# RWKV recurrence: four more two-bank products copied out of PSUM by ScalarE and VectorE, one bank each

## What is computed

```python
def step(state, inp):                      # per token, 4 heads of 64
    r_t, w_t, k_t, v_t, kk_t, b_t = inp
    sa = jnp.einsum("bhvk,bhk->bhv", state, -kk_t)
    state = (state * w_t[:, :, None, :] + sa[..., None] * b_t[:, :, None, :]
             + v_t[..., None] * k_t[:, :, None, :])
    y_t = jnp.einsum("bhvk,bhk->bhv", state, r_t)
    return state, y_t
_, y = lax.scan(step, s0, (tm(rh), tm(wh), tm(kh), tm(vh), tm(kk), tm(bh)))
ym = jnp.mean(y, axis=-1, keepdims=True)
yv = jnp.mean(jnp.square(y - ym), axis=-1, keepdims=True)
y = (y - ym) * lax.rsqrt(yv + GN_EPS) * gn_w + gn_b
```

## Time and profile before

| | |
|---|---|
| runs | 2478.01, 2481.12, 2484.82 us |
| profiled execution | 2481.37 us, span 2479.6 us, mean granted clock 0.923 |
| RWKV recurrence in it | about 455 to 696 us |
| busy in the whole span | TensorE 87%, VectorE 34%, ScalarE 24%, GpSimd 9% |

### The profile page before, as it was taken

The page is one execution under the profiler, slowest core; times in us unless marked ns, Lnnn a source line. Parts: engine busy times, 40 slices in busy tenths (PEclk is TensorE's granted clock), DMA queues, the critical chain, the costliest instruction groups (busy, mean ns, idle before and its releaser), DMA issues. The chain is left out here.

```text
span 2479.6 us, 27540 instructions
## 1 busy us (share of the span) xinstructions
PE 2155.0 (87%) x10876; PEld 1246.0 (50%) x10876; DVE 845.3 (34%) x1865; ACT 591.3 (24%) x1404; POOL 211.5 (9%) x305
## 2 busy tenths in 40 slices
PE   8999986468789784999996899999999949999990
PEld 4545542267634663444442565677674424444440
DVE  0115444466605434212112453344351141121115
ACT  1013323153301220111112343333331111111112
POOL 0000001201125110000000100000000000000002
PEclk9999988688889896999998899999999969999995
DMA  3500000000021116999996300000010047999956
GB/s 119 204 22 35 18 1 0 3 2 3 3 103 51 56 51 246 347 367 372 361 375 238 123 3 1 1 1 1 1 69 28 34 179 291 366 375 363 370 232 222
DMA packets 46200, 349.30 MB, mean 141 GB/s; under 512 B 6256, under 2 KB 6576, under 8 KB 36208
## 3 DMA queue, kind: packets, MB, share of 16 engines
q1 hardware_dynamic: 32176, 296.97, 30.8%
q0 software_dynamic: 13888, 50.47, 5.9%
HBM read 292.82 MB, written 54.59 MB: 140 GB/s over the span
## 5 line engine op out<-in xcount | busy, mean ns | idle before, releaser
L202 PE MATMUL psum<-arena 128*128 128x512 f32 (+7 forms) x9328 | 1990.3, 393 | 204.1 <-DVE arena L1901 25.9
L202 PEld LDWEIGHTS psum<-arena 128*128 128x128 f32 (+3 forms) x9328 | 1068.2, 176 | 1057.4 <-issue 879.6
L2032 DVE TENSOR_TENSOR arena<-psum,arena 128x256 f32<-128x256 f32 x64 | 27.2, 425 | 540.2 <-ACT arena L2076 540.2
L2110 POOL DMA_INDIRECT arena<-xn_rows,arena x64 | 60.2, 941 | 820.3 <-PE psum L1999 588.2
L2076 ACT ACTIVATE arena<-psum 128x256 f32<-128x256 f32 x64 | 24.7, 386 | 408.3 <-PE psum L202 408.3
L1455 ACT ACTIVATE arena<-arena 128x1024 f32<-128x1024 f32 x43 | 45.4, 1056 | 259.5 <-DVE arena L2744 101.6
L2657 ACT ACTIVATE arena<-psum,arena 128x1024 f32<-128x1024 f32 (+8 forms) x72 | 50.3, 700 | 188.5 <-DVE arena L2693 188.5
L1161 ACT ACTIVATE arena<-psum 64x256 f32<-64x256 f32 (+4 forms) x176 | 67.1, 389 | 115.4 <-PE psum L202 82.2
L2069 ACT ACTIVATE arena<-psum 128x512 f32<-128x512 f32 x64 | 38.3, 598 | 185.5 <-PE psum L202 185.5
L1999 PE MATMUL psum<-arena 128*128 128x128 f32 x512 | 68.2, 277 | 10.8 <-DMA arena<-xn_rows,arena 10.8
L1999 PEld LDWEIGHTS psum<-arena 128*128 128x128 f32 x512 | 59.2, 144 | 12.2 <-DMA arena<-xn_rows,arena 11.1
(11 more groups left out here) (290 smaller groups left out, 1336.1 us busy)
## 6 DMA issues: line engine op xcount, KB each, us to landing
arena<-in_w_exp SPq DMA_DIRECT2D x64, 3072.0 KB, 11.7
expert_rows<-arena SPq DMA_DIRECT2D x80, 512.0 KB, 3.8
arena<-in_x SPq DMA_DIRECT2D x16, 512.0 KB, 5.2
xn_rows<-arena SPq DMA_DIRECT2D x16, 512.0 KB, 2.6
arena<-in_w_out SPq DMA_DIRECT2D x8, 512.0 KB, 7.3
arena<-in_w_o SPq DMA_DIRECT2D x1, 4096.0 KB, 13.2
out<-arena SPq DMA_DIRECT2D x8, 512.0 KB, 2.7
arena<-in_rows SPq DMA_DIRECT2D x6, 512.0 KB, 6.6
```

What stands on the lines that cost most here:

```text
L202: return e.matmul(out, lhsT, rhs, start=start, stop=stop, skip_group_check=True)
L2110: e.indirect_dma_start(out=xe, out_offset=None, in_=xn_dram[:, :], in_offset=bass.IndirectOffsetOnAxis(idx.bitcast(I32)[:, block:block + 1 ...
```

## The change

Chunk 1 of p8, xt, q32 and q64 goes from ScalarE to VectorE. In the list FRONT their second entries become "V". ScalarE's steps 4, 6, 7 and 9 copy chunk 0 only. VectorE's helper `chunk1` takes a width, and is called in step 4 ahead of the combination x2, and in new steps 6, 7 and 9. That is 4 copies of 64x256 fewer per tile for ScalarE and 4 more for VectorE, 32 in all; matmuls, masks and combinations are as before.

```diff
         FRONT = [...
-                 ("p4_0", "S"), ("p4_1", "V"), ("x1_0", "V"), ("x1_1", "V"), ("p8_0", "S"), ("p8_1", "S"), ("x2_0", "V"), ("x2_1", "V"),
-                 ("akv_0", "S"), ("akv_1", "S"), ("x3_0", "V"), ("x3_1", "V"), ("xt_0", "S"), ("xt_1", "S"), ("q32_0", "S"), ("q32_1", "S"),
-                 ("pb_0", "V"), ("pb_1", "V"), ("q64_0", "S"), ("q64_1", "S")]
+                 ("p4_0", "S"), ("p4_1", "V"), ("x1_0", "V"), ("x1_1", "V"), ("p8_0", "S"), ("p8_1", "V"), ("x2_0", "V"), ("x2_1", "V"),
+                 ("akv_0", "S"), ("akv_1", "S"), ("x3_0", "V"), ("x3_1", "V"), ("xt_0", "S"), ("xt_1", "V"), ("q32_0", "S"), ("q32_1", "V"),
+                 ("pb_0", "V"), ("pb_1", "V"), ("q64_0", "S"), ("q64_1", "V")]
...
                 elif s == 4:
-                    for c in range(2):
-                        chunk(fr, "p8", c, own["P1"][:, 0], 4)
+                    chunk(fr, "p8", 0, own["P1"][:, 0], 4)
...
                 elif s == 6:
-                    for c in range(2):
-                        chunk(fr, "xt", c, own["X1"][:, 0], 4)
+                    chunk(fr, "xt", 0, own["X1"][:, 0], 4)
                 elif s in (7, 9):
-                    for c in range(2):
-                        chunk(fr, "q32" if s == 7 else "q64", c, Q, 4)
+                    chunk(fr, "q32" if s == 7 else "q64", 0, Q, 4)
...
-                def chunk1(name, dst):
+                def chunk1(name, dst, n=8):
                     key = (i, f"{name}_1")
                     e.wait_ge(*fr.full(key))
-                    e.tensor_copy(flat(dst)[HALVES[1]], side(fr.bank[key], HALVES[1], 8)).then_inc(*fr.drain(key, "V"))
+                    e.tensor_copy(dst[HALVES[1]], side(fr.bank[key], HALVES[1], n)).then_inc(*fr.drain(key, "V"))
...
                 elif s == 4:
+                    chunk1("p8", own["P1"][:, 0], 4)
                     for c in range(2):
                         e.wait_ge(*fr.empty((i, f"x1_{c}")))
                     combine(fr, "x2", X2[:, 1], X1[:, 1], ALU.add)
...
+                elif s == 6:
+                    chunk1("xt", X1[:, 0], 4)
+                elif s in (7, 9):
+                    chunk1("q32" if s == 7 else "q64", own["Q"], 4)
```

More of the change, by code:

```diff
@@ L1252, in dve_rwkv @@
                     e.tensor_tensor(X2[:, 1], own["T3"][:, 0], bc_mid(id64, 4), ALU.add).then_inc(*V.up())
-                    chunk1("p2", own["P1"])
+                    chunk1("p2", flat(own["P1"]))
                 elif s == 2:
@@ L1258, in dve_rwkv @@
                 elif s == 3:
-                    chunk1("p4", own["P2"])
+                    chunk1("p4", flat(own["P2"]))
                     e.wait_ge(*V.last())
```

## The result

| | before | changed |
|---|---|---|
| median of 15 runs | 2482.60 us (2476.47 to 2485.58) | 2490.62 us (2484.75 to 2495.43) |
| ratio, with 95% interval | | 1.0032 (1.0023 to 1.0042) |
| span of the profiled execution | 2479.6 us | 2490.0 us |

The kernel became 8.0 us slower by the medians, 10.4 us in the two profiled executions. The interval straddles the 0.3% that I had named as the border between slower and no change.

What follows compares the result with a forecast made beforehand. It took the RWKV recurrence's chain through TensorE and the engines emptying PSUM as the bound. Queueing at q64 6.6, clock 1.4 and first tile 0 made +8.0 us on 2481.4: 2489.4 us, range 2484.6 to 2493.2.

Steps and rivals of the forecast that it cites:

- The price of a copy: New VectorE copy of 64x256 from PSUM: 0.43 us, hardly above 0.69.
- p8 in steady tiles: VectorE's p8 copy fits its wait for x2 with 0.02 us to spare: cost 0, up to 0.05 a tile.
- xt, q32: Split copies of xt and q32 let pb come 0.16 to 0.28 us earlier; 0.20 taken.
- q64: Second bank's copy waits behind VectorE's reciprocal and product: x64 1.14 us later, net 0.94 a tile, 6.6 over seven.
- The clock: Longer idleness behind q64 pushes steady tiles to the lower granted clock: 0 to 3.4 us, 1.4 taken.
- the two kinds of tiles: Steady tiles of before: 21.9 to 22.2 us at mean clock 0.92, 22.9 to 23.4 at 0.85.
- rival 1: q64's second copy is not held up on VectorE: 3.6 us faster, 2477.8 us; chance 0.05.
- The first tile: With RG-LRU steps in VectorE's queue, x64's combination waits for VectorE anyway: 0, from -0.3 to +0.5 us.
- Rival 3: Every tile mostly at the lower clock, perhaps p8 delays x2: +10.6 us, 2492.0 us; chance 0.20.
- Rival 4: Part of the q64 delay is absorbed, half left: +3.5 to 4 us, 2485.2 us; chance 0.10.
- The rules: For: use ScalarE and VectorE to empty PSUM. Against: their queues are strictly first in, first out. No size given.

Runs made afterwards that it cites:

- the pair with filled gaps: Extra matmuls around q64 in tiles 1 to 7: changed kernel with 24 and 30, 2479.94 us (0.9998); kernel before with 24 and 14, 2470.66 us (0.9963).
- gaps_filled_before: Kernel before with 24 extra matmuls behind pb and 14 behind q64 in tiles 1 to 7; 2470.66 us, ratio 0.9963.
- step19_behind: Changed kernel with VectorE copying q64's second bank ahead of the previous tile's reciprocal and product; 2478.90 us, ratio 1.0001.
- xt_q32_split: Kernel before with only xt and q32 split over both engines, p8 and q64 on ScalarE; 2469.59 us, ratio 0.9957.
- q64_on_scalar: Changed kernel with both banks of q64 given back to ScalarE, p8, xt and q32 still split; 2473.10 us, ratio 0.9979.
- only_p8_split: Kernel before with p8 alone split over both engines; 2479.74 us, ratio 0.9996.

## Why the prediction was right, and where not

The forecast was 2489.4 us, +8.0; measured are 2490.62, +8.0 against the fresh median of before. The mechanism is shown, by the rows of the changed kernel and by undoing and doing q64 alone. That the two numbers agree to the decimal is luck: the interval of the ratio reaches from 5.7 to 10.4 us. The sum is also partly right by compensation: in the profiled pair the seven steady tiles give 7.5 us (5.9 + 1.6), where I had 6.6 + 1.4 = 8.0, and the first tile gives 2.6, where I had 0.

- *The price of a copy.* 0.43 was worked out; 0.427 to 0.428 is what line 1236 shows.
- *p8 in steady tiles.* Right: they cost nothing. The hole was a little less narrow than forecast: the copy ends at 649.25 and x2's combination starts at 649.42, where I had 0.02 to spare, since the copy overlaps the end of the step ahead of it.
- *xt, q32.* 0.20 was taken; 0.19 measured.
- *q64.* x64 was to start 1.14 us later after the reciprocal; it does, to 0.01. Seven tiles pay; the six between reciprocals gave 5.9 in the profiled pair against 5.6 from the queue alone.
- *The clock.* I took 1.4 us, from the difference of the two kinds of tiles in the earlier trace rows. One more tile of six was of the slower kind, about 1 us by that reckoning, and the pair with filled gaps gives about 1 as well. Right in size, but the view was too narrow: both kinds already had the half clock in them. A tile of before without it takes 20.8 at its shortest (gaps_filled_before), 1.1 to 2.6 less than those in the earlier trace rows. I also wrote that more idleness can only push tiles to the slower kind; step19_behind has more idleness around q64 and x64 than before and fewer slow tiles (last section). So rival 1 was priced too low: xt_q32_split has only its upstream part, 0.2 a tile, and gains 9.0.
- *The first tile.* I counted 0 and bounded it at 0.5, looking only at its end, where x64's combination waits for VectorE. I never walked p8's copy through the RG-LRU steps: it delays x2, the third step of line 959 and with it the RG-LRU matmuls, 0.45 us, before the place at which I began. In the profiled pair the tile is 2.6 longer. For the medians its price is open, as said.
- *Rival 3* (all tiles at the lower clock, 2492.0) was nearer to the profiled execution (four of six tiles, 2491.7) than to the median. *Rival 4* (absorbed, half of it left) is out: at the full clock the shortest tiles differ by 0.9 of the 0.94, the mean ones by 0.79. *The rules:* using both engines to empty PSUM paid for xt and q32, where VectorE was idle, and cost at q64, where it wasn't; the in-order queue decides which.

## What to carry to other kernels

Before a copy is given to a second engine, read what that engine's program has in front of it at the moment when the product is full, not how busy it is on average: VectorE was idle for a third of each tile and still made q64 1.14 us late, seven times. Moving the obstacle only moves the wait, if a later step of the same chain needs the same engine before the obstacle is done.

Where TensorE waits in many short gaps, compare with a tile that runs at the full clock, made by filling the gaps with matmuls whose result nobody uses if there is none in the trace. That tells at once what the clock is worth, and which small saving might bring it back.

## What was not expected of the hardware

- With 0.2 us less waiting per tile the half-speed stretches are gone from most steady tiles of the profiles: 20.6 to 20.7 us at 1.00 in four of six in q64_on_scalar and five of six in xt_q32_split, against 21.9 to 23.4 at 0.92 or 0.85 before. The six tiles are 10.1 and 10.7 us shorter, where 6 x 0.2 is 1.2; the medians of the whole kernels moved by 5.8 and 9.0. In both kernels TensorE still stands for 1.64 and 0.88 us around q64, so the size of these gaps alone doesn't decide it; what does was not isolated. Nor is it all or nothing: only_p8_split, whose steady chain waits as that of before does, has one tile of six at 1.00 (21.4 us), and the runs of before themselves spread from 2472.6 us at a mean clock of 0.929 to 2485.8 at 0.922 (the 29 runs beside q64_on_scalar, whose own have 0.927 to 0.929). Only one execution of before was traced, so how many of its tiles run at the full clock in its fast runs is not known.
- step19_behind has 0.57 and 0.98 where before has 0.88 ahead of x64, thus more waiting in all, and four of its six tiles run at the full clock (130.3 us for six, against 135.6). In this pair the sum of the gaps did not decide the clock.
- Matmuls that compute nothing, 38 a tile, made the kernel before 8.9 us faster (0.9963).
